# Mixer output stage of an encoder layer: the output projection's weights loaded and split in the first token block only

## The reference, cut to what matters

```python
# D_MODEL = 1024, SEQ = 2048, float32
g = sigmoid(...)                              # two gates of SEQ x D_MODEL
a_branch = fourier_mix(u_f) @ w_fa            # (2048 x 512) @ (512 x 1024)
n_branch = neighbourhood_attention(q, k, v, rpb) @ w_nb
mixed = g[:, :, 0] * a_branch + g[:, :, 1] * n_branch
x = x + mixed @ w_out                         # (2048 x 1024) @ (1024 x 1024)
h2 = rms_norm(x, norm2_g)                     # input of the feed-forward
...
```

## Time and profile before

| | |
|---|---|
| median of 3 runs | 3146.33 us (3138.73 to 3149.79) |
| the profiled execution's own time | 3149.32 us |
| its span, first to last instruction | 3147.4 us |
| mean granted clock of TensorE | 0.963 of full speed |
| PE busy / POOL busy / DVE busy | 91% / 22% / 38% of the span |
| mixer output phase | about 1186 to 1640 us of the span |

### The profile page before, as it was taken

How to read it: one execution, slowest core, us unless ns; L and a number is a source line. 1 busy time by engine, 2 the same in 40 slices (tenths; PEclk the granted TensorE clock), 3 DMA queues, 4 the chain that set the end, 5 groups by cost and what they waited for, 6 DMA issues and landing times. The chain is left out here.

```text
span 3147.4 us, 33077 instructions
## 1 busy us (share of the span) xinstructions
PE 2873.8 (91%) x13320; PEld 2361.9 (75%) x13320; DVE 1209.0 (38%) x1656; ACT 677.6 (22%) x1254; POOL 703.6 (22%) x293
## 2 busy tenths in 40 slices
PE   7999999993549996998879999999999998999998
PEld 6888888883548884776767888888888887888886
DVE  5200000004549885456534232323232323464564
ACT  4211111111236650211123111111111111111011
POOL 1010101012112315345412001100110011444442
PEclk9999999997769998999989999999999999999999
DMA  4321212113286736566643101110111013554543
GB/s 142 92 85 68 69 68 77 67 70 116 74 182 162 185 92 201 189 199 194 200 139 130 54 27 54 54 54 27 54 54 54 31 51 123 178 196 151 197 171 107
DMA packets 179704, 349.22 MB, mean 111 GB/s; under 512 B 59253, under 2 KB 80497, under 8 KB 173425
## 3 DMA queue, kind: packets, MB, share of 16 engines
q1 hardware_dynamic: 160624, 330.55, 32.9%
q10 hardware_dynamic: 18944, 16.78, 1.6%
HBM read 257.03 MB, written 91.78 MB: 111 GB/s over the span
## 5 line engine op out<-in xcount | busy, mean ns | idle before, releaser
L1644 PE MATMUL ff_psum<-ff_h,ff_w 128*128 128x512 f32 x4224 | 988.6, 395 | 17.7 <-DVE ff_h L1484 16.6
L1644 PEld LDWEIGHTS ff_psum<-ff_h,ff_w 128*128 128x128 f32 x4224 | 791.2, 187 | 215.1 <-POOL ff_w L1446 14.9
L1446 POOL TENSOR_TENSOR ff_w<-ff_wraw,ff_w 128x1024 fp32r<-128x1024 f32 x132 | 318.6, 2414 | 1190.3 <-DVE ff_w L1478 1190.3
L357 PE MATMUL in_psum<-in_hT,in_w 128*128 128x512 f32 x2304 | 522.6, 389 | 0.0
L357 PEld LDWEIGHTS in_psum<-in_hT,in_w 128*128 128x128 f32 x2304 | 432.6, 188 | 89.6
L1664 PE MATMUL ff_psum<-ff_w,ff_hid 128*128 128x512 f32 x2112 | 481.6, 391 | 9.3 <-DVE ff_hid L1502 9.1
L1664 PEld LDWEIGHTS ff_psum<-ff_w,ff_hid 128*128 128x128 f32 x2112 | 397.9, 188 | 92.9 <-issue 10.1
L1257 PE MATMUL mo_psum<-mo_act,mo_w 128*128 128x512 f32 x768 | 196.4, 412 | 59.4 <-POOL mo_w L1102 37.9
L1257 PEld LDWEIGHTS mo_psum<-mo_act,mo_w 128*128 128x128 f32 x768 | 147.9, 197 | 105.6 <-POOL mo_w L1102 47.9
L202 POOL TENSOR_TENSOR in_w<-in_wraw,in_w 128x1024 fp32r<-128x1024 f32 x32 | 77.1, 2413 | 620.4 <-DVE in_w L279 310.7
L1490 DVE SCALAR_TENSOR_TENSOR ff_gate<-ff_psum,ff_param,ff_gate 128x2047 f32<-128x2047 f32 x22 | 51.7, 2350 | 372.9 <-ACT ff_gate L1585 372.9
(11 more groups left out here) (119 smaller groups left out, 2393.5 us busy)
## 6 DMA issues: line engine op xcount, KB each, us to landing
ff_wraw<-in_w_down_dram SPq DMA_DIRECT2D x88, 512.0 KB, 3.3
ff_wraw<-in_w_up_dram SPq DMA_DIRECT2D x44, 512.0 KB, 5.8
hidden<-ff_val SPq DMA_DIRECT2D x22, 1024.0 KB, 4.9
ff_kraw<-hidden SPq DMA_DIRECT2D x44, 512.0 KB, 4.5
at_bias<-shifted SPq DMA_DIRECT2D x72, 256.0 KB
in_wraw<-in_w_in_dram SPq DMA_DIRECT2D x32, 512.0 KB, 3.7
gT<-in_stage SPq DMA_DIRECT2D x64, 256.0 KB, 2.4
mo_wraw<-in_w_mix_dram SPq DMA_DIRECT2D x32, 512.0 KB, 3.8
```

Of the source, the lines that this page charges most:

```text
L357: last = nc.tensor.matmul(ps[:, bank], w[:, a, s, k], hT[:, c, k, b * BLK:(b + 1) * BLK], start=(k == 0 and (a, c) == SPLIT[0]), stop=(k = ...
L1446: nc.gpsimd.tensor_tensor(w[:, 1, n % RING], wraw[:, n % RAW], f32(w[:, 0, n % RING]), ALU.subtract).then_inc(w_tail, 1)
L1644: last = nc.tensor.matmul(ps[:, 4 * (t % 2) + b], w[:, a, t % RING, k * P:(k + 1) * P], h[:, c, k, b * BLK:(b + 1) * BLK], start=(k == 0 a ...
```

## The change

In block 0 nothing is changed: its list alternates the two kinds of tile as before. In blocks 1 to 3 the list holds `w_mix` tiles only, and PE reads the `w_out` heads and tails that block 0 left in `wo`. The places in the list are noted when it is built (`mix_at`, `out_at`), and `loads(b, s)` says how many tiles a step handles. PE waits for `w_out` tiles only in its first output tile, and DVE's wait before it overwrites `wo` is gone.

```diff
-        order = [("mix", 0)]
+        order, mix_at, out_at = [("mix", 0)], [0], []
         for b in range(NBLK):
             for s in range(KD):
                 if s < KD - 1 or b < NBLK - 1:
+                    mix_at.append(len(order))
                     order.append(("mix", (s + 1) % KD))
-                order.append(("out", s))
-        def w_index(b, kind, s):
...
+                if b == 0:
+                    out_at.append(len(order))
+                    order.append(("out", s))
+
+        def loads(b, s):
+            return (s < KD - 1 or b < NBLK - 1) + (b == 0)
...
-                    if s < KD - 1 or b < NBLK - 1:
+                    for _ in range(loads(b, s)):
                         load_w()
-                    load_w()
...
-                    w_tails(2 if s < KD - 1 or b < NBLK - 1 else 1)
+                    w_tails(loads(b, s))
...
                     else:
-                        at_least(dve, out_mm, 2 * TPB * b)
                         dst = wo[:, 0, :, t]
...
-                    w_heads(b, s, 2 if s < KD - 1 or b < NBLK - 1 else 1)
+                    w_heads(b, s, loads(b, s))
...
-                pe.wait_ge(w_tail, w_index(b, "mix", s) + 1)
+                pe.wait_ge(w_tail, mix_at[n] + 1)
...
-                    if t == 0:
-                        pe.wait_ge(w_tail, w_index(b, "out", (half + 1) * SPH - 1) + 1)
+                    if n == 0:
+                        pe.wait_ge(w_tail, out_at[(half + 1) * SPH - 1] + 1)
```

## The result

The changed kernel took 3117.91 us (median of 4 runs, 3114.26 to 3119.15), the kernel before beside it 3144.22. By these ratios it is 27 to 29 us faster. The forecast was 3117.7 us and 28.6 us faster, with a range of 3106 to 3129.

The account below looks back on a forecast made before the run. PE was taken to wait in the mix stage of blocks 1 to 3 for a DVE and POOL chain holding w_out work. Gains 24.0 + 3.4 + 1.2 = 28.6 us off 3146.33 gave 3117.7 us, range 3106 to 3129.

Parts of the forecast that it names:

- steps 2 to 7: Mix stage of blocks 1 to 3, step 2 to output stage: 18 steps at 5.65 us replace 125.7 us, gain 24.0.
- What bounds the step: Mix stage, blocks 1 to 3: PE waits at the end of a 7.22 us step for DVE and POOL, delayed by w_out.
- The raw ring: Weight loads: two raw places serve two kinds of tile, so w_mix in effect has one raw place.
- Limit (a): Mix step, PE itself: 24 matmuls at 0.2355 us each take 5.65 us, which sets the new step.
- Limit (b): Mix step, DVE and POOL chain: two steps take at least 10.87 us, one 5.44, under PE's 5.65 by 0.21.
- Rival 1: Mix-stage add still meets POOL: two steps 11.98 us, gain 22.5, time 3123.8; chance 0.16 with rival 3's milder case.
- Limit (c): Mix step, w_mix load behind two gate tiles: landing taken as 4.4 us, 5.7 allowed, hidden with 1.3 to spare.
- rival 3: Mix-stage w_mix load replaces the wait: about 3153 us, chance 0.03; milder case 3129, chance 0.16 with rival 1.
- Start of the output stage: Blocks 1 and 2: PE's wait for the last mix tails goes, gain 3.4 us, bounds 0 and 3.5.
- Step 1's tail: Start of mix stage, blocks 1 to 3: POOL's tail takes 2.36 us, not 2.80; gain 1.2, bounds 0 and 1.4.
- Slow clock: Block 1's stretch within six steps goes; those in the first step of blocks 2 and 3 stay, 3.0 us if gone.
- Rival 2: Fewer slow-clock stretches in blocks 2 and 3 and 5.58 us steps: gain 32.9, time 3113.4; chance 0.16.

Follow-up runs that it names:

- e2: Changed kernel with GpSimd's w_out subtraction put back in blocks 1 to 3, into an unread tile; ratio 0.9936 to the kernel before.
- e5: Changed kernel with VectorE's w_out cast put back in blocks 1 to 3, into an unread tile; ratio 0.9924 to the kernel before.
- e3: Changed kernel with the 24 w_out loads put back in blocks 1 to 3, into an unread tile; ratio 0.9928 to the kernel before.
- e6: Changed kernel with both w_out cast and subtraction put back in blocks 1 to 3, without loads; ratio 0.9948 to the kernel before.
- e4: Kernel before, with a raw place of its own for w_out tiles, leaving two for w_mix; ratio 0.9996 to the kernel before.
- e1: Changed kernel with the next w_mix load issued ahead of the gate tiles in blocks 1 to 3; ratio 0.9893 to the kernel before.
- e9: The changed kernel itself measured again with more runs; 3120.54 against 3150.27 us, ratio 0.9909 to the kernel before.
- e8: Changed kernel with e1's load order, next block's activation tiles and step 1's w_mix tile split earlier; 3102.01 us, ratio 0.9850 to the kernel before.
- e10: e8 with block 0's w_out casts on ScalarE instead of VectorE; 3094.42 us, ratio 0.9837 to the kernel before.
- e7: Kernel before, with the w_out cast on ScalarE instead of VectorE; ratio 0.9985 to the kernel before.

## Why the prediction was right

The total was right within a microsecond, and the mechanism was right in the main. That the total is so near is luck in part: two errors in steps 2 to 7 cancel, and the kernel before, taken as 3146.33 us, had a median of 3144.22 beside the changed one, so that the gain by the ratio was 27.0 and not 28.6. By its own steps:

- *What bounds the step.* Right: PE waited for a chain in which the `w_out` work of GpSimd and VectorE stood. e2, e5 and e3 put back one part each: 9.6, 2.5 and 6.8 us of steps, and e6 two parts, 15.1. The two halves of the split lengthen each other, since 9.6 + 2.5 = 12.1 is less than 15.1. Split and loads add up: 15.1 + 6.8 = 21.9, and all together are 22.1 (125.7 less 103.6). The prediction gave nothing to the traffic of the loads; by e3's profile that was wrong, the 12.6 MB cost 6.8 us on their own, about 3.3 of it by the slow clock behind the longer waits.
- *The raw ring.* The prediction said that `w_mix` had in effect one raw place. It had, but e4 shows that this alone set nothing: with two places for `w_mix` the regular step stayed at 7.22 us.
- *Limit (a), PE's own step.* 5.65 us forecast, 5.49 measured (0.229 us a matmul, not 0.2355): 18 x 0.16 = 2.9 us better than summed. The x48 group at 1434.15 wasn't free of waits, as the prediction took it to be. Its second step began 0.05 us after the end of GpSimd's tail, and the row of the weight loads shows the wait that the matmuls' row doesn't list:

```profile
1439.88 5.31 PEld L1257 LDWEIGHTS mo_psum<-mo_act,mo_w 128*128 128x128 f32 x24 [0.42 <-POOL mo_w L1102]
```

- *Limit (b), the chain.* The forecast of 0.68 for the add (0.69 in the median) and of two steps in 10.87 us held as a bound; the waits over 1 us in the changed kernel's steps are of the late load and not of it. But it was nearer than 0.21 us a step: 10.87 / 2 = 5.44 against PE's 5.49, and in e1 GpSimd's tail ends 0.13 to 0.20 us before PE begins steps 4 to 7. Nor were the adds of blocks 1 to 3 all at 0.69: 17 of the 24 were, and seven met GpSimd for a moment and took 0.77 to 1.13 us. Rival 1, with adds of 1.8 us and a step of 5.99, didn't occur, and e2 shows what it would have been like.
- *Limit (c), the load.* This is the term that failed. The landing time was taken as 4.4 us from the gates' row; it is 5.8 in the median, and 6.8 in the step shown. By the same formula (11.3 + 6.8) / 3 is 6.0 us a step, and with PE's 5.49 the load may take only 5.2. In block 1 VectorE's cast began 0.66 us after the tile of step 3 had landed, 0.06 after that of step 4, and waited 1.64 for that of step 5: the load falls behind step by step, and once per block PE waits 1.3 to 1.4 us. These waits, and the somewhat longer steps next to them, are the 5.1 us that e1 got back. The sum for steps 2 to 7 was 24.0, measured 21.9 to 22.1: 2.9 more from (a), 5 less from (c). It was the milder case of rival 3, at a smaller size than its 3129 us.
- *Start of the output stage.* 3.4 forecast, 4.0 measured. *Step 1's tail.* 1.2 forecast, 1.3 measured.
- *Slow clock.* The two stretches within steps 2 to 7 of before, in blocks 1 and 3, went, and are about 3 of the 21.9 us. The prediction named only the one of block 1, but the sum had both in it. It left the stretches in step 1 in; they stayed, 1.65 us longer in the first profile of the changed kernel and 1.5 us shorter in e9's, which is scatter. Rival 2 didn't occur. In the Trainium skill, TensorE: Matmul & The Clock Gate, section HAM oscillation, waits between bursts let the clock fall; the traces agree in part. In the ten profiles with the stall ahead of step 1 the clock fell at step 1 in 18 of their 30 later blocks (in none of e6's three, in all of e3's, e4's and e5's), and in none of the six of e8 and e10, where the stall is gone. What decides it where the stall is there stays open.
- *Feed-forward and phases ahead.* No edit and no effect that stands out of their scatter (6.2 and 1.1 us).

The expectations of e6 and e7 failed for one reason: the 7.22 us step was taken to be GpSimd and VectorE alone, and the transfers were left out. Its regular length needs the `w_out` transfer too, which makes the cast late enough to fall between the two subtractions (e6), and behind it the `w_mix` load is the next limit (e7). How the 15.1 us of the split divide further between contention and queue can't be given as one sum, since the two halves lengthen each other.

## What to carry to other kernels

Work that never sat on PE's queue (24 subtractions, 24 casts, 24 loads) was worth 27 us, because it took turns with the chain that PE waited for: price such a removal by the step that is left, from the next limit, not by the durations removed. Write down every limit of the new step, and take a transfer's landing time from an issue with the same neighbours ahead of it; a limit that passes by a small margin deserves its own check, since here the load was forecast with 1.3 us to spare, and moving its issue ahead of two others was worth 5 us of steps. When an edit gives nothing (e4), look in the trace whether the wait that it was meant to remove is gone; and when it is gone and the time is nearly the same (e7), look for the wait that took its place.

## What the runs showed of the hardware that was not expected

- VectorE's `tensor_tensor` with two SBUF inputs (128 x 512), begun under a GpSimd subtraction, ends 0.54 to 0.56 us after it in all 95 cases of before, the changed kernel and e6, however early it began; in e2, begun 0.03 us behind one of 2.39 us, it took 2.92. The 32 casts of weight tiles (128 x 1024) that begin under one in before end 0.55 to 0.69 us after it. That looks like being held until GpSimd's instruction ends, and not like being slowed. The Trainium skill, GPSIMD Engine Reference, section Key points, speaks of contention with instructions that have two SBUF inputs; the traces agree for the add and the mix tail.
- The multiplies, with one input in PSUM, took 0.67 to 0.69 us with GpSimd running or not (one at 1435.50 in e2 took 0.68, with a subtraction begun at 1435.66).
- A `w_mix` tile of 512 KB landed in 4.1 us in the median when it was issued ahead of the gate tiles (e1) and in 5.8 behind them (the changed kernel), with the same bytes per step.
